# A two-layer diffusion-step kernel on one core: weight loads issued from another queue, half as many small table loads, and half of the expert output gathered inside the last expert chunk

## The reference, cut to what matters

```python
for l in range(DEPTH):                                   # 2 layers
    sh1, sc1, gt1, sh2, sc2, gt2 = modulation(cond, w_ada[l], b_ada[l])   # cond @ w_ada: 1024 x 6144
    mix = mixer(adaln(x, norm_attn[l], sh1, sc1), ...)   # attention and delta rule, then w_out
    x = residual(x, gt1, mix)                            # x + gt1 * mix
    # routed_moe: top 2 of 16 experts for a token, y = sum over both of gate * expert(h)
    x = residual(x, gt2, routed_moe(adaln(x, norm_ffn[l], sh2, sc2), ...))
```

## Time and profile before

| | us |
|---|---|
| median of 3 runs (lowest, highest) | 1893.29 (1893.01, 1895.04) |
| the profiled execution, its own time | 1897.15 |
| its span, first to last instruction | 1895.4 |
| PE busy | 1631.1 (86%) |
| DVE busy | 1207.6 (64%) |
| ACT busy | 932.4 (49%) |
| POOL busy | 242.2 (13%) |
| mean granted clock of TensorE | 0.932 of full speed |

### The profile page before, as it was taken

How to read it: one execution, slowest core, us unless ns; L and a number is a source line. 1 busy time by engine, 2 the same in 40 slices (tenths; PEclk the granted TensorE clock), 3 DMA queues, 4 the chain that set the end, 5 groups by cost and what they waited for, 6 DMA issues and landing times. The chain is left out here.

```text
span 1895.4 us, 32729 instructions
## 1 busy us (share of the span) xinstructions
PE 1631.1 (86%) x11909; PEld 1325.4 (70%) x11910; DVE 1207.6 (64%) x1728; ACT 932.4 (49%) x1438; POOL 242.2 (13%) x361
## 2 busy tenths in 40 slices
PE   3998886799895999999949989789979679999992
PEld 0798675687553888888838986678855468888881
DVE  1478453556346996996664883646654579899664
ACT  2254642233323886886543445323341278888651
POOL 0000035111000111111020000541200011111112
PEclk7899998999896999999969999879999889999996
DMA  8241356654305997997553110665331489999754
GB/s 339 78 151 48 100 153 163 189 178 143 137 34 205 412 405 294 380 408 269 211 218 112 56 48 1 174 197 157 95 129 53 167 304 402 408 397 409 296 198 178
DMA packets 186803, 392.96 MB, mean 207 GB/s; under 512 B 88682, under 2 KB 106114, under 8 KB 161094
## 3 DMA queue, kind: packets, MB, share of 16 engines
q1 hardware_dynamic: 163374, 326.12, 47.7%
q10 hardware_dynamic: 14824, 34.39, 4.6%
q0 software_dynamic: 8496, 30.94, 4.3%
HBM read 345.95 MB, written 45.45 MB: 207 GB/s over the span
## 5 line engine op out<-in xcount | busy, mean ns | idle before, releaser
L2363 DVE TENSOR_TENSOR expert_w_lo<-shared,expert_w_hi 128x2048 fp32r<-128x2048 f32 x192 | 433.4, 2287 | 58.3 <-ACT expert_w_hi L2302 58.3
L2302 ACT ACTIVATE expert_w_hi<-shared 128x2048 fp32r<-128x2048 f32 x192 | 366.5, 1913 | 44.1 <-PEq L146 39.6
L2229 PE MATMUL ps<-expert_w_hi,expert_x_hi 128*128 128x512 f32 x592 | 245.2, 414 | 11.0 <-DVE expert_x_lo L2358 9.2
L2231 PE MATMUL ps<-expert_w_hi,expert_x_lo 128*128 128x512 f32 x592 | 233.2, 394 | 0.0
L2230 PE MATMUL ps<-expert_w_lo,expert_x_hi 128*128 128x512 f32 x592 | 233.1, 394 | 0.0
L2229 PEld LDWEIGHTS ps<-expert_w_hi,expert_x_hi 128*128 128x128 f32 x592 | 113.5, 192 | 42.5 <-issue 12.9
L2231 PEld LDWEIGHTS ps<-expert_w_hi,expert_x_lo 128*128 128x128 f32 x592 | 112.3, 190 | 24.3
L2230 PEld LDWEIGHTS ps<-expert_w_lo,expert_x_hi 128*128 128x128 f32 x592 | 112.8, 191 | 18.7
L2284 PE MATMUL ps<-expert_w_hi,expert_hid_hi 128*128 128x512 f32 x296 | 115.8, 391 | 0.5 <-ACT expert_hid_hi L2337 0.5
L2199 POOL COPY expert_cur_idx<-slot_tokens 128x1 int32 x37 | 48.4, 1307 | 530.2 <-PE ps L2216 530.2
L2285 PE MATMUL ps<-expert_w_lo,expert_hid_hi 128*128 128x512 f32 x296 | 115.3, 390 | 0.0
(11 more groups left out here) (380 smaller groups left out, 3376.7 us busy)
## 6 DMA issues: line engine op xcount, KB each, us to landing
shared<-in_w_up SPq DMA_DIRECT2D x64, 1024.0 KB, 7.4
shared<-in_w_down SPq DMA_DIRECT2D x64, 1024.0 KB, 9.4
shared<-in_w_gate SPq DMA_DIRECT2D x64, 1024.0 KB, 8.3
qkv<-in_w_ada SPq DMA_DIRECT2D x20, 1280.0 KB, 6.1
shared<-in_w_in SPq DMA_DIRECT2D x10, 2048.0 KB, 9.2
y_table<-expert_y ACTq DMA_DIRECT2D x37, 512.0 KB, 8.5
qkvT<-in_w_ada SPq DMA_DIRECT2D x20, 768.0 KB, 8.5
setup_ada_ring<-in_w_ada SPq DMA_DIRECT2D x8, 1024.0 KB, 12.2
```

What stands on the lines that cost most here:

```text
L2229: pe.matmul(bank, x_hi[:, at], w_hi[:, j, w], start=(q == 0), stop=False)
L2231: return pe.matmul(bank, x_lo[:, at], w_hi[:, j, w], start=False, stop=(q == KD - 1))
L2302: act.activation(w_hi[:, j, :], raw[:, j, :], ACT.Copy).then_inc(w_hi_done, 1)
L2363: dve.tensor_tensor(w_lo[:, j, :], raw[:, j, :], w_hi[:, j, :].bitcast(F32), ALU.subtract).then_inc(w_lo_done, 1)
```

## The change

Five edits. (1) The next unit's two loads are issued by ACT, right behind `take(n)`, and no longer by SP. (2) A table entry now holds one direction of a tile, and entries are ordered so that both directions of a step lie side by side: X and Y take two DMAs of 128 KB each in place of four of 64 KB, QK and the corner one in place of two; `base_b` loads stay four. (3) For i = 2 SP runs `scatter(0)`, `x_load(0)` and `y_load(0)` ahead of `base_load(3)`. (4) In the expert phase POOL, after all raw weights are split and all y but the last chunk's are stored, gathers first-slot rows: tiles 0 and 1 in layer 0 (into the weight buffer's piece 5), all five in layer 1. In the last chunk DVE waits for `gate_in` and adds tiles 0 and 1 to x, two instructions of 128x1024 for each, ahead of its copy of y. (5) `Joined` then gathers 8 tiles, needs no `act_first` for tiles 0 and 1, and its `dve_sum` for them has two instructions; `combine_phase` gathers 5 tiles, ACT has no part in it, and DVE first adds the first-slot rows of tiles 2 to 4, then the second-slot rows of all five, two instructions each.

```diff
-BASE = 2 * 4 * 2 * (HB * HB + HB)
+BASE = 4 * 2 * (HB * HB + HB)
...
+EARLY = 2
...
     def gathers(self, pool):
         for t in range(NT):
-            for n in range(2):
+            for n in range(int(t < EARLY), 2):
                 pool.indirect_dma_start(out=self.place(t, n), out_offset=None, in_=self.A.y_table,
                                         in_offset=bass.IndirectOffsetOnAxis(ap=self.R.slots[:, n, t:t + 1], axis=0))\
                     .then_inc(self.got[t], 16)
         for t in range(NT):
-            pool.wait_ge(self.got[t], 32)
+            pool.wait_ge(self.got[t], 16 if t < EARLY else 32)
...
+        g, w = G.gate_view[:, int(t > 0), :], self.R.gates[:, 1, t:t + 1]
         if t == 0:
...
-        dve.wait_ge(self.first, t + 1)
-        dve.scalar_tensor_tensor(out=b, in0=b, scalar=self.R.gates[:, 1, t:t + 1], in1=a,
-                                 op0=ALU.mult, op1=ALU.add).then_inc(self.both, 1)
-        dve.wait_ge(self.both, t + 1)
-        dve.tensor_tensor(b, b, G.gate_view[:, int(t > 0), :], ALU.mult).then_inc(self.gated, 1)
+        if t < EARLY:
+            dve.wait_ge(self.got[t], 16)
+            dve.scalar_tensor_tensor(out=b, in0=b, scalar=w, in1=g, op0=ALU.mult, op1=ALU.mult).then_inc(self.gated, 1)
+        else:
+            dve.wait_ge(self.first, t - EARLY + 1)
+            dve.scalar_tensor_tensor(out=b, in0=b, scalar=w, in1=a, op0=ALU.mult, op1=ALU.add).then_inc(self.both, 1)
+            dve.wait_ge(self.both, t - EARLY + 1)
+            dve.tensor_tensor(b, b, g, ALU.mult).then_inc(self.gated, 1)
         dve.wait_ge(self.gated, t + 1)
         dve.tensor_tensor(G.x[:, t, :], G.x[:, t, :], b, ALU.add).then_inc(self.added, 1)
...
+class FirstHalf:
+    def __init__(self, ph, G, A, l, R):
+        self.G, self.A, self.R = G, A, R
+        self.tiles = range(EARLY if l + 1 < DEPTH else NT)
+        at = 5 * PIECE if l + 1 < DEPTH else 0
+        self.rows = G.carve(at, (len(self.tiles), D))
+        self.got = [ph.dma_sem(G.soft[f"y_early{t}"]) for t in self.tiles]
+        self.scaled, self.summed = ph.sem("early_scaled"), ph.sem("early_summed")
+    def gathers(self, pool):
+        for t in self.tiles:
+            pool.indirect_dma_start(out=self.rows[:, t, :], out_offset=None, in_=self.A.y_table,
+                                    in_offset=bass.IndirectOffsetOnAxis(ap=self.R.slots[:, 0, t:t + 1], axis=0)).then_inc(self.got[t], 16)
+    def dve_sum(self, dve, t):
+        G, a = self.G, self.rows[:, t, :]
+        dve.wait_ge(self.got[t], 16)
+        dve.scalar_tensor_tensor(out=a, in0=a, scalar=self.R.gates[:, 0, t:t + 1], in1=G.gate_view[:, int(t > 0), :],
+                                 op0=ALU.mult, op1=ALU.mult).then_inc(self.scaled, 1)
+        dve.wait_ge(self.scaled, t + 1)
+        dve.tensor_tensor(G.x[:, t, :], G.x[:, t, :], a, ALU.add).then_inc(self.summed, 1)
...
                 if joined:
-                    for t in range(2):
-                        joined.act_first(act, t)
                     joined.act_stats(act, 0)
                     joined.act_first(act, 2)
                     joined.act_stats(act, 1)
...
-    def load_after(self, sp, n):
+    def load_after(self, act, n):
         i = self.of_pair(n)
         if i is not None and i + 1 < len(self.todo):
-            sp.wait_ge(self.done, i + 1)
-            self.load(sp, i + 1)
+            act.wait_ge(self.done, i + 1)
+            self.load(act, i + 1)
...
+        def place(i, d):
+            g = group(i)
+            first, n = (0, 1, 3)[g], (1, 2, 2)[g]
+            return 2 * first + d * n + i - first
+        def both(table, s, size):
+            a, b = (place(ORDER.index(t), d) for d, t in enumerate(tiles(s)))
+            return table[0:2 * NT * size].rearrange("(f x) -> f x", x=size)[a:b + 1:b - a]
+        def mine(table, i, size):
+            return table[0:2 * NT * size].rearrange("(f x) -> f x", x=size)[place(i, 0):place(i, 1) + 1:place(i, 1) - place(i, 0)]
+        def entry(table, at, n=1):
+            return table[at * BASE:(at + n) * BASE]
...
-                    sp.dma_start(A.qk_table[i], QKF[i].rearrange("p d h n -> p (d h n)")).then_inc(s_["qk_out"], 16)
+                    sp.dma_start(paired(mine(A.qk_table, i, P * DH * P)), QKF[i].rearrange("p d h n -> p d (h n)")).then_inc(s_["qk_out"], 16)
...
                 def bl_load(s):
                     sp.wait_ge(s_["t1l_p"], s)
-                    for d in range(2):
-                        sp.dma_start(flat(BtL)[half(d)], A.corner[place(s, d), half(d)]).then_inc(s_["bl_in"], 16)
+                    sp.dma_start(flat(BtL), both(A.corner, s, HB * DH * HB).rearrange("f (r n) -> f r n", r=HB)).then_inc(s_["bl_in"], 16)
...
-                    for d in range(2):
-                        sp.dma_start(QK[:, d].rearrange("p h n -> p (h n)"),
-                                     A.qk_table[place(s, d), :, d * DH * P:(d + 1) * DH * P]).then_inc(s_["qk_in"], 16)
+                    sp.dma_start(QK.rearrange("p d h n -> p d (h n)"), paired(both(A.qk_table, s, P * DH * P))).then_inc(s_["qk_in"], 16)
...
                     for d in range(2):
-                        sp.dma_start(small(A.base_x, i, d), (Rt if d else R)[p, d]).then_inc(base_out[group(i)], 16)
-                        sp.dma_start(small(A.base_y, i, d), (R if d else Rt)[p, d]).then_inc(base_out[group(i)], 16)
+                        at = 2 * step_of(i, d) + d
+                        sp.dma_start(small(entry(A.base_x, at)), (Rt if d else R)[p, d]).then_inc(base_out[group(i)], 16)
+                        sp.dma_start(small(entry(A.base_y, at)), (R if d else Rt)[p, d]).then_inc(base_out[group(i)], 16)
...
                 def x_load(s):
-                    sp.wait_ge(base_out[group(place(s, 0))], 64 if s == 0 else 128)
+                    sp.wait_ge(base_out[group(ORDER.index(tiles(s)[0]))], 64 if s == 0 else 128)
                     if s:
                         sp.wait_ge(s_["t1l_p"], s)
-                    for d in range(2):
-                        for b in range(2):
-                            sp.dma_start(X[half(b), d], large(A.base_x, place(s, d), b)[:, d * DH:(d + 1) * DH]).then_inc(s_["xy_in"], 16)
+                    for b in range(2):
+                        sp.dma_start(eight_of(X, b), large(entry(A.base_x, 2 * s, 2), b)).then_inc(s_["xy_in"], 16)
                 def y_load(s):
                     if s:
                         sp.wait_ge(s_["yf_done"], at(s - 1, 1))
-                    for d in range(2):
-                        for b in range(2):
-                            sp.dma_start(Y[half(b), d], large(A.base_y, place(s, d), b)[:, d * DH:(d + 1) * DH]).then_inc(s_["xy_in"], 16)
+                    for b in range(2):
+                        sp.dma_start(eight_of(Y, b), large(entry(A.base_y, 2 * s, 2), b)).then_inc(s_["xy_in"], 16)
...
                     if i + 1 < FRONT:
                         front_out(i + 1)
+                        if i == 2:
+                            scatter(0)
+                            x_load(0)
+                            y_load(0)
                         base_load(i + 1)
-                    units.load_after(sp, i)
-                    if i == 2:
-                        scatter(0)
-                        x_load(0)
-                        y_load(0)
                     units.store_after(sp, i)
                 for s in range(NT):
                     m = FRONT + PER * s
-                    units.load_after(sp, m)
                     if s < 2:
                         scatter(2 * s + 1)
                         scatter(2 * s + 2)
...
                         bl_load(s + 1)
                         x_load(s + 1)
                         y_load(s + 1)
-                    units.load_after(sp, m + 1)
                     units.store_after(sp, m + 1)
                     if s == 1:
                         sp.wait_ge(s_["st_done"], at(0, 1))
                         sp.dma_start(A.new_state[0, l:l + 1].rearrange("a d h k v -> k (a d) h v"), S[:, 0]).then_inc(s_["s_out"], 16)
-                    units.load_after(sp, m + 2)
...
-                                pe.wait_ge(s_["xy_in"], 128 * (s + 1))
+                                pe.wait_ge(s_["xy_in"], 64 * (s + 1))
...
                     act.wait_ge(s_["pt_p"], n + 1)
                     act.activation(pT[:, :, 0:nk], G.ps[:, 6:8, 0:nk], ACT.Copy).then_inc(s_["pt_taken"], 1)
+                    units.load_after(act, n)
...
+                pool.wait_ge(w_lo_done, NE * PIECES)
+                pool.sem_inc(passed, 1)
+                pool.wait_ge(y_out, total * 16)
+                pool.sem_inc(passed, 1)
+                half.gathers(pool)
                 pool.wait_ge(gathered, total * 16 + 16)
                 pool.sem_inc(passed, 1)
+                for t in half.tiles:
+                    pool.wait_ge(half.got[t], 16)
...
                         if m == 0 and not (last and final):
                             take(k + 1, 1)
```

(46 more changed lines are left out.)

41 lines of the change are left out of this document (23 added, 18 removed).

## The result

The changed kernel takes 1914.56 us (median; 1910.64 to 1917.78) where the kernel before took 1893.15 in the same runs. The ratio is 1.011 (95% interval 1.0088 to 1.0132). The prediction was 1898.5, with a range of 1886 to 1908: the sign was that of the likeliest case, the size was 4 times too small, and the time lies above the range.

What follows compares the result with a forecast made beforehand. PE's waits in the mixers and DVE's final chain were taken as the bound. Terms +19.1 (layer 0's mixer), +5.4, -12.5, +0.3 and -6.9 sum to +5.4 on 1897.15; set to the median, 1898.5 us, range 1886 to 1908.

Steps and rivals of the forecast that it cites:

- the likeliest case: Whole kernel: the forecast itself, 1898.5 us, own range 1895 to 1903, slower than before; chance 0.42.
- X and Y before step 0: Mixer starts: the scatter and loads issued earlier take about 6 us off layer 0 and 3.4 off layer 1.
- rival B: Mixers: a unit on the other ring delays scatters and X, Y loads; +9.5 us, 1908; chance 0.15.
- The third term of B: Layer 1's mixer: the 3.1 us wait for X and Y before step 1 stays.
- the units behind the take: Layer 0's mixer: loads issued late; six waits sum to 33.6 us for 15.7 before, 17.9 more.
- the clock's 7.2 us: Layer 0's mixer: longer waits at pairs 9, 11, 14 and 17 lower the clock, 1.8 us each.
- rival C: Layer 0's mixer: the waits come as worked out but without the clock's 7.2 us; 1891; chance 0.19.
- rival A: Layer 0's mixer: loads take 8.0 us and the clock holds, so 11.1 us go; 1887; chance 0.24.
- Layer 1's mixer: Layer 1: 12.5 us less: start 3.4, pair 5's wait 3.5, slow matmuls 2.5, step 1's wait 3.1.
- the last chunk of layer 0: End of layer 0's experts: store 8.8 us later waiting for gate rows, 3.4 given back; net 5.4 more.
- The combine phase: End of the program: sixteen DVE instructions, six ahead needing no gather, end at 1884.5 for 1891.53; 6.9 us less.
- layer 1's last chunk: End of layer 1's experts: the early sums fit DVE's idle time; 0.3 us more, bounds 0 and 3.

Runs made afterwards that it cites:

- e3: Changed kernel without the first-slot gathers and sums in layer 0's last chunk, layer 1's kept: 1907.64 us, ratio 1.0059.
- e14: Changed kernel with only the corner store split into two DMAs of 64 KB: 1905.51 us, ratio 1.0055.
- e15: Changed kernel with the unit load behind pair 3 left out in both layers: 1872.2 us, but tokens go to other experts, so only the mixers compare.
- e9: e2 with the corner store split into two DMAs, one for each direction: 1885.41 us, ratio 0.9944 to the kernel before.
- e13: Changed kernel, unit loads behind the exponentials, corner store in two, gate rows first, the load behind pair 3 on SP behind Y: 1861.48 us, ratio 0.9808.
- e1: Kernel before with only the units' loads moved from SP to ACT behind the take: 1911.68 us, ratio 1.0084.
- e8: Kernel before with only the new table layout, its loads, stores and counts: 1899.57 us, ratio 1.0025.
- e2: Changed kernel with the units' loads back on SP at their old places: 1900.03 us, ratio 1.0020 to the kernel before.
- e5: Changed kernel with the units' loads still on ACT but behind the pair's exponentials, not behind the take: 1878.44 us, ratio 0.9899.
- e11: Kernel before with only the early first-slot gathers and sums and the shorter Joined and combine sums: 1896.89 us, ratio 0.9998.
- e10: e11 with SP loading the gate rows ahead of the next layer's first weights and modulation rows: 1887.13 us, ratio 0.9943.
- e7: Kernel before with only scatter(0), x_load(0) and y_load(0) moved ahead of base_load(3): 1897.2 us, ratio 1.0001.

## Why the prediction was wrong, by its own steps

**The step that failed: X and Y before step 0.** The prediction took 6.0 us off layer 0 and 3.4 off layer 1. From the start of the mixer PE reached step 0 2.4 us later in layer 0 and 5.1 later in layer 1 (49.2 for 46.85, 51.05 for 45.94): 8.4 and 8.5 us of miss. All stages together miss by 13.6 (19.0 - 5.4), since others came out some 3 better, most of it the 2.4 of layer 1's experts, which is chance. Two causes are shown, and this table of PE's start of step 0, counted from the mixer's start, tells what each is worth:

| | layer 0 | layer 1 |
|---|---|---|
| before | 46.9 | 45.9 |
| forecast | 40.9 | 42.5 |
| changed kernel | 49.2 | 51.1 |
| e3, the same mixers | 51.4 | 50.9 |
| e14, corner store in two | 48.1 | 47.5 |
| e15, no unit beside X and Y | 46.1 | 44.6 |
| e9, both, units on SP | 42.0 | 42.7 |
| e13, both, units behind the exponentials | 40.4 | 41.4 |

One cause out gives back at most 3.2 of the 8.4 us in layer 0 and 6.4 of the 8.5 in layer 1. With both out PE comes within 1.1 us of the forecast (e9) or ahead of it (e13). Those two runs move other units too, so the shares of the two are not separated further.

First, the unit's load on ACT's queue catches the scatter or the X and Y loads (e1, e15). The prediction had this as rival B, at a chance of 0.15, and priced it too low: it let 4 of the 6.0 us go, and 2.4 of the 3.4, where all was lost and more. (The third term of B, 3.1 us before step 1, was wrong the other way: that wait is gone.) The argument "the landing, 297.85 - 295.3 = 2.5 before, about as much" took a landing from a moment when no unit was in flight, and rows 3 showed no DMA beside a unit from another queue; the unit's own 9.5 us in place of the 2.5 would have given 298 in layer 0, for the 299.5 that came. Nor did the forecast ask what the unit before would do to SP's stores and scatter: X went out at 290.31 and not at 285.8, behind issues of 2.49 (corner store) and 2.26 us (scatter) beside a unit that landed at 284.1. On such sharing the Trainium skill (DMA: Bandwidth & Descriptors, "Issuing engines are not separate DMA queues") says that DMAs of all issuing engines interleave on the same 16 DMA engines. The runs agree, with 3.0 us alone (e15) and 7.0 beside a unit (the changed kernel).

Second, a term was missing. The text costed the corner loads, hidden behind a step, and never the corner store, for which SP waits inside `base_load`. Edit 2 alone, with this store in it, cost 4.7 us (e8); splitting the store gave 9 in the changed kernel (e14) and 14.6 in e2 (e9). The store's DRAM side now begins with the two directions, where both sides began with 128 rows. Why that is slow the runs don't show by themselves, only that one DMA of 64 rows for each direction isn't. The Trainium skill gives a reason (DMA: Bandwidth & Descriptors, "Why a DMA increments its semaphore by 16 and not by 1"): the number of DMA engines that share a transfer is the largest, up to 16, that divides the size of the slowest dimension of either side. By that it would be 2 here, an estimate from this page; no trace here shows how many took part, and the times of e9 and e14 fit it.

**Right: the units behind the take.** Six waits at the six pairs named, 35.8 for 33.6 us; none at pair 5. e5 shows the reason to be the place behind `take`. The sum is closer than its terms, which miss by up to 1.7 us either way (8.24 for 6.7 at pair 6, 7.18 for 5.5 at pair 9, 4.57 for 5.6 at pair 17). Of the clock's 7.2 us, the rest of layer 0's mixer leaves 4.6 (27.0 less 2.4 for X and Y and 20.0 for the units from pair 5 on); this is an estimate, with whatever else changed there in it. All four newly long waits, at pairs 9, 11, 14 and 17, were followed by 2.36, as said. "Only the clock holds" (rival C) and "quick loads" (rival A) fall with it: the second part of a load landed 7.9 to 11.7 us after its issue in layer 0's mixer, 9.3 in the median of the six that PE waited for, where the forecast took 8.15.

**Layer 1's mixer.** Behind step 0 the forecast had 9.1 us less (3.5, 2.5 and 3.1), and 8.5 came: both waits are gone. The same mixers differ by 3 us from one profile to another, so this tells no more than that the size is right. The 3.4 of the start became a loss of 5.1.

**Right: the last chunk of layer 0 and the end.** +9.7 and -4.6 for +8.8 and -3.4; the gathers cost 2.7 and not 1.8. The combine phase gave 7.2 for 6.9, and layer 1's last chunk takes 16.4 us before and after. e11 shows that the edits 4 and 5 together are worth nothing (the forecast's terms for them sum to -1.2), e10 that the price of the first was the order of SP's loads.

**Edit 3** alone shortens the wait by 3.6 and 2.9 us at the named place and nothing in time (e7): the prediction counted a gain at one wait without asking what PE would meet sooner behind it.

## What to carry to other kernels

When an issue moves to another engine's program, find the instruction that it now stands behind and the one that wants its data: that gave this case's large term, 33.6 us of waits for the 35.8 measured, and moving the same load a few instructions up turned a loss of 1.1% into a gain of 1.0%. A small transfer that another queue's large one may catch is to be priced at up to the large one's duration: here 7.0 to 9.4 us where the unit took 7.9 to 9.7. And it can be caught at each link of a chain (stores, scatter, load). Of a layout change price every DMA that touches the table, its stores and who waits for them too, with an eye on the outermost dimension.

## What was not expected of the hardware

Two DMAs of 128 KB that land in 3.0 us with no unit beside them take 7.0 to 9.4 beside 2 MB from another queue, and an issue on SP that takes 0.49 us took up to 4.54 while a unit was in flight. A store of 128 KB whose outermost dimension in DRAM is 2 had SP wait until 4.5 us after its issue; in e14 SP went on 1.5 us after the issue of two stores of 64 rows (266.68 to 268.15). A wait of 2.37 us (pair 5 in e9) was followed by matmuls of 2.36, one of 2.58 in the kernel before by 1.30. The granted clock was at full speed when either wait began; it fell to 0.50 at the end of the first and stayed at 1.00 through the second. So the length of the wait alone doesn't tell at which of its two levels the granted clock will stand; the runs here don't settle what does.
